# Mixing the last two KV heads of dilated attention: branch weights as 12 rows spread by TensorE in place of rows broadcast by DMA, results left on chip, h fetched last, last maxima fetched by SyncE

## The reference, cut to what matters

```python
for g, (win, dil) in enumerate(BRANCHES):          # ((128, 1), (512, 4), (2048, 16))
    if kv_past is None:
        o, l = dilated_prompt(q[:, :, g], kv_branches[g], win, dil)
    else:
        o, l = dilated_sample(q[:, :, g], kv_branches[g], kv_past[g], win, dil)
    outs.append(o)
    lses.append(l)
wts = jax.nn.softmax(jnp.stack(lses, axis=0), axis=0)
o = jnp.einsum('gnth,gnthe->nthe', wts, jnp.stack(outs, axis=0))
return o.reshape(n, t, ATTN_OUT).astype(h.dtype) @ w_o
```

## Time and profile before

| | |
|---|---|
| median of 3 runs | 2897.13 us (2895.83 to 2897.22) |
| the profiled execution | 2900.13 us, span 2898.4 us |
| TensorE busy | 2710.8 us, 94% of the span |
| VectorE busy | 1365.3 us, 47% |
| ScalarE busy | 832.7 us, 29% |
| sample phase: from the first sample scores to the product with `w_o` | 1884.2 to 2027.0 us, 142.8 us |
| mean granted TensorE clock | 0.958 of full speed |

### The profile page before, as it was taken

One profiled execution on the slowest core, in us unless ns is written; L12 is line 12 of the kernel. 1 busy time (PEld: TensorE's weight loads), 2 busy tenths in 40 slices (PEclk: granted clock), 3 DMA queues, 4 the chain that ended last, 5 costly groups with the idle time before them and its releaser, 6 DMA issues.

```text
span 2898.4 us, 44440 instructions
## 1 busy us (share of the span) xinstructions
PE 2710.8 (94%) x18658; PEld 2577.6 (89%) x18658; DVE 1365.3 (47%) x2255; ACT 832.7 (29%) x1680; POOL 285.0 (10%) x464
## 2 busy tenths in 40 slices
PE   5589999999999999999999999775999999999998
PEld 4489999999999999988888888554999999999998
DVE  8972145423332335666667667534255333233325
ACT  7221132111111113245554544512131111111112
POOL 2300000000000000012422424321000000000000
PEclk8689999999999999999999999867999999999999
DMA  3412111111111111323344454668211111111101
GB/s 95 79 35 59 44 44 44 44 44 43 43 43 43 44 57 53 97 62 84 84 108 129 106 132 112 224 172 272 81 44 44 46 54 40 49 43 43 43 29 61
DMA packets 175567, 215.54 MB, mean 74 GB/s; under 512 B 45894, under 2 KB 128310, under 8 KB 175160
## 3 DMA queue, kind: packets, MB, share of 16 engines
q1 hardware_dynamic: 152960, 161.32, 18.6%
q0 software_dynamic: 22464, 52.23, 7.1%
HBM read 164.86 MB, written 29.92 MB: 67 GB/s over the span
## 4 chain that ended last, share of the span: by engine, by line
PE 73%; DVE 7%; DMA 4%; ACT 3%; issue 3%; POOL 2%; DVEq 0%; POOLq 0%; ACTq 0%
PE PS L221 11%; PE PS L218 11%; PE PS L217 11%; PE PS L396 8%; PE PS L400 8%; PE PS L397 8%; PE PS L2075 4%; PE PS L2076 3%; PE PS L2077 3%; PE PS L2090 2%; DMA CB<-C_SCRATCH 2%; PE PS L2117 2%; PE PS L2104 1%; DVE SQ L191 1%; DVE SSB L2002 1%
## 5 line engine op out<-in xcount | busy, mean ns | idle before, releaser
L217 PE MATMUL PS<-XH,WH 128*128 128x352 f32 x1920 | 617.6, 322 | 3.7 <-PEq L103 3.7
L218 PE MATMUL PS<-XL,WH 128*128 128x352 f32 x1920 | 619.1, 323 | 0.0
L396 PE MATMUL PS<-HIDH,WH 128*128 128x352 f32 x1536 | 494.7, 323 | 8.1 <-DVE HIDL L331 8.1
L397 PE MATMUL PS<-HIDL,WH 128*128 128x352 f32 x1536 | 494.5, 323 | 0.0
L221 PE MATMUL PS<-XH,WL 128*128 128x352 f32 x1920 | 415.0, 324 | 0.0
L217 PEld LDWEIGHTS PS<-XH,WH 128*128 128x128 f32 x1920 | 362.4, 189 | 4.2 <-issue 4.1
L218 PEld LDWEIGHTS PS<-XL,WH 128*128 128x128 f32 x1920 | 361.3, 188 | 0.1
L347 DVE TENSOR_TENSOR H<-PS,H 128x1056 f32<-128x1056 f32 x128 | 160.8, 1256 | 391.6 <-PE PS L400 391.2
L400 PE MATMUL PS<-HIDH,WL 128*128 128x352 f32 x1536 | 331.6, 324 | 0.0
L221 PEld LDWEIGHTS PS<-XH,WL 128*128 128x128 f32 x1920 | 329.4, 188 | 0.0
L396 PEld LDWEIGHTS PS<-HIDH,WH 128*128 128x128 f32 x1536 | 289.2, 188 | 12.7 <-DVE HIDL L331 12.7
(11 more groups left out here) (367 smaller groups left out, 3461.9 us busy)
## 6 DMA issues: line engine op xcount, KB each, us to landing
RAW<-w_up SPq DMA_DIRECT2D x32, 1024.0 KB, 5.3
RAW<-w_down SPq DMA_DIRECT2D x32, 1024.0 KB, 4.9
KVR<-cache_kv_w SPq DMA_DIRECT2D x18, 1024.0 KB, 10.2
QB<-QA SPq DMA_DIRECT2D x120, 132.0 KB, 2.5
ARAW<-w_q SPq DMA_DIRECT2D x24, 512.0 KB, 4.7
O_SCRATCH<-OT POOLq DMA_DIRECT2D x96, 128.0 KB, 2.8
OB<-O_SCRATCH POOLq DMA_DIRECT2D x24, 512.0 KB, 7.0
CB<-C_SCRATCH POOLq DMA_DIRECT2D x48, 256.0 KB, 8.3
```

Of the source, the lines that this page charges most:

```text
L217: nc.tensor.matmul(out, wh(k), xh[:, k, c], start=(k == 0), stop=False)
L218: nc.tensor.matmul(out, wh(k), xl[:, k, c], start=False, stop=False)
L396: nc.tensor.matmul(out, w, m.hidh[:, k, q], start=(k == 0), stop=False)
L397: nc.tensor.matmul(out, w, m.hidl[:, k, q], start=False, stop=False)
```

## The change

Only the mixing of `g` = 2 and 3 (pairs `w` = 4 to 7, now 12 pieces `p`, piece `p` being branch `p % 3` of pair `4 + p // 3`) and what stands around it is changed:

- The weight tile in DRAM is loaded as rows of 512 columns into `CR_RAW` (`pool_rows`: six small loads, 12 rows and, again for the part that full precision loses, 12 more for each half of the columns). ScalarE and VectorE split them into a high and a low part in `CR` (`act_rows`, `dve_rows`). For each piece TensorE multiplies a selection matrix `SEL` with them (`pe_spread`), which spreads a pair's two rows over 128 partitions in a PSUM bank, 2 or 7, half the columns at a time. VectorE multiplies `OB` with the bank (`dve_piece`). The two `CB` loads of each branch are gone.
- Sums of `w` = 4 to 7 stay on chip (`CB` for 4 and 5, `XF` for 6 and 7) and are split from there; their stores to `X_SCRATCH` and loads from it are gone.
- Step by step the pieces stand at steps 0, 1, 2, 4, 5, 6 (`PIECES`), two each. The maxima of `g` = 3 are loaded by SyncE and not by GpSimd, and VectorE uses them at the end of step 1 (before: step 0), the weights at the end of step 2.
- `choose(u-1)` stands before `score(u+1)` and no longer behind the product with V; `keep_o(u-1)` opens VectorE's step. Keys are turned through two banks, and the sample results use bank 6 alone, since banks 2 and 7 are for the pieces.
- SyncE waits only for the last projection before it loads the first five cache tiles, and for the last rotation (`roped`) before the masks. The three `QBL` memsets go from VectorE (steps 84 to 86) to GpSimd (85 to 87). `h` is fetched after `w_o` and later.
- One cache tile (`KVR2`) moves by 512 bytes, and the last tile of step 7 lies in it.

```diff
+    LATE = 2
+    BANKS = (2, 7)
...
+        if g <= self.LATE:
+            self.load_maxima(pool, g, self.ml_in)
+
+    def load_maxima(self, eng, g, sem):
...
     def pool_weights(self, pool, g):
         pool.wait_ge(self.kept, g + 1)
         pool.dma_start(self.s.cd[g], self.s.ct[:]).then_inc(self.ct_out, 16)
-        pool.wait_ge(self.ct_out, 16 * (g + 1))
+        if g < self.LATE:
+            pool.wait_ge(self.ct_out, 16 * (g + 1))
...
+    def adds(self, p):
+        return 2 * (p // 3) + p % 3
+
+    def acc(self, w):
+        return self.s.cb[:, w - 4] if w < 6 else self.s.xf[:, w, 0:SEQ]
+
+    def pool_rows(self, pool, g, free, count):
+        pool.wait_ge(self.ct_out, 16 * (g + 1))
+        pool.wait_ge(free, count)
+        rows = self.s.cd[g].rearrange("(k r) i -> k (r i)", r=8)
+        for e in range(2):
+            for y, n in ((0, 12), (12, 12), (24, 8)):
+                pool.dma_start(self.s.cr_raw[32 * e + y:32 * e + y + n, :], rows[0:n, 512 * e:512 * e + 512]).then_inc(self.rows_in, 16)
+
+    def act_rows(self, act, g):
+        act.wait_ge(self.rows_in, 96 * (g - 1))
+        if g == 3:
+            act.wait_ge(self.spread, 12)
+        self.nc.scalar.activation(self.s.cr[:], self.s.cr_raw[:], ACT.Copy).then_inc(self.row_hi, 1)
...
+    def pool_piece(self, pool, p):
+        s, w, b = self.s, 4 + p // 3, p % 3
+        if p < 2:
+            pool.wait_ge(self.weighed, 11 + p)
+        else:
+            pool.wait_ge(self.taken, 2 * p - 2)
+            pool.wait_ge(self.mixed, self.adds(p - 2))
+        pool.dma_start(s.ob[:, p % 2], s.od[w // 2, b][:, w % 2].rearrange("p t q -> p (t q)")).then_inc(self.b_in[p % 2], 16)
+
+    def pe_spread(self, pe, p):
+        w, b = 4 + p // 3, p % 3
+        pair = 2 * b + w % 2
+        pe.wait_ge(self.rows, w // 2 - 1)
+        for e in range(2):
+            if p:
+                pe.wait_ge(self.taken, 2 * p - 1 + e)
+            rows = slice(32 * e, 32 * e + 24)
+            self.nc.tensor.matmul(self.m.ps[:, self.BANKS[e], :], self.s.sel[rows, pair, :], self.s.cr[rows, :],
+                                  start=True, stop=True).then_inc(self.spread, 1)
+
+    def dve_piece(self, dve, p, free, n):
+        w, b = 4 + p // 3, p % 3
+        acc, ob = self.acc(w), self.s.ob[:, p % 2]
+        dve.wait_ge(self.b_in[p % 2], 48 * 6 + 16 * (p // 2 + 1))
...
+        for e in range(2):
+            dve.wait_ge(self.spread, 2 * p + e + 1)
+            c = self.m.ps[:, self.BANKS[e], :]
...
+            self.nc.vector.tensor_tensor(x if b else half_tiles(acc, b, 0, e), x, c, ALU.mult).then_inc(self.taken, 1)
+        if b:
+            dve.wait_ge(self.taken, 2 * p + 2)
+            dve.wait_ge(self.mixed, self.adds(p) - 1)
+            v = by_tile(acc, b, 0)
+            self.nc.vector.tensor_tensor(v, v, by_tile(ob, b, 1), ALU.add).then_inc(self.mixed, 1)
...
-        if c >= 3:
-            pe.wait_ge(self.kept[self.by_dve(c - 3)], self.before(c - 3))
+        if c >= 2:
+            pe.wait_ge(self.kept[self.by_dve(c - 2)], self.before(c - 2))
...
+PIECES = {0: (0, 1), 1: (2, 3), 2: (4, 5), 4: (6, 7), 5: (8, 9), 6: (10, 11)}
...
     def _(pool):
-        mix.pool_part(pool, 0, 3)
-        for g in (2, 3):
-            for x in range(12 if g == 3 else 13, 31):
-                mix.pool_part(pool, x, g)
+        mix.pool_rows(pool, 2, mix.made, 3)
+        mix.pool_maxima(pool, 3)
+        for p in range(2, 8):
+            mix.pool_piece(pool, p)
+        mix.pool_weights(pool, 3)
+        mix.pool_rows(pool, 3, mix.rows, 1)
+        for p in range(8, 12):
+            mix.pool_piece(pool, p)
...
+            if u in (0, 4):
+                mix.act_rows(act, 2 + u // 4)
             act.wait_ge(neg, u + 1)
...
-        act.wait_ge(pv, 8)
+        act.wait_ge(pv, 7)
         for k in range(KT):
-            act.wait_ge(x_in, 16 * 6 if k < 6 else 16 * 8)
-            nc.scalar.activation(m.xl[:, k, 0:SEQ], s.xf[:, k, 0:SEQ], ACT.Copy).then_inc(x_hi, 1)
-            if k == 0:
+            if k < 4:
+                act.wait_ge(x_in, 16 * 4)
+            else:
+                act.wait_ge(mix.mixed, 2 * (k - 3))
+            nc.scalar.activation(m.xl[:, k, 0:SEQ], result(k), ACT.Copy).then_inc(x_hi, 1)
+            if k == 5:
                 act.wait_ge(placed, 8)
                 nc.scalar.activation(m.xl[:, :, SEQ:NT], s.at_s[:], ACT.Copy).then_inc(s_hi, 1)
```

More of the change, by code:

```diff
@@ L1528, in __init__ @@
         self.weighed, self.added = sig("weighed"), sig("added")
+        self.rows_in, self.row_hi, self.rows, self.sel_made = sig("rows_in"), sig("row_hi"), sig("rows"), sig("sel_made")
+        self.ml_late = sig("ml_late")
+        self.spread, self.taken, self.mixed = sig("spread"), sig("taken"), sig("mixed")
     def pool_maxima(self, pool, g):
@@ L1626, in pool_part @@
             self.pool_maxima(pool, g)
+        elif x == 12 and g == self.LATE:
+            self.pool_weights(pool, g)
+            self.pool_piece(pool, 0)
+            self.pool_piece(pool, 1)
         elif x == 12:
@@ L2155, in sample_phase, with result @@
         "p_turned", "kept_p", "pv", "kept_o", "picked", "placed", "pick_set"))
[L2156 removed]
+    pick_zero, x_in, s_hi, x_hi, x_lo, s_lo = (sig(n) for n in ("pick_zero", "x_in", "s_hi", "x_hi", "x_lo", "s_lo"))
+    s.s_lo = s_lo
     s.h_in, s.x_lo, s.masked, s.kept_p = sig("h_in"), x_lo, masked, kept_p
     tile, tiles = keys_s.tile, keys_s.tiles
+    def result(k):
+        return s.xf[:, k, 0:SEQ] if k < 4 else mix.acc(k)
     def kt(u, n, j, x):
@@ L2185, in _ @@
                     load(u, j)
-            if u < 2:
-                mask(u)
+            if u == 1:
+                sp.wait_ge(s.roped, 3 * N_GR)
+                mask(0)
+                mask(1)
         load(4, 0)
@@ L2292, in place, with low @@
             ins.then_inc(placed, 1)
+        def low(k):
+            dve.wait_ge(x_hi, k + 1)
+            nc.vector.tensor_tensor(m.xh[:, k, 0:SEQ], result(k), f32(m.xl[:, k, 0:SEQ]), ALU.subtract).then_inc(x_lo, 1)
+        mix.dve_choice(dve)
         for u in range(8):
+            if u:
+                keep_o(u - 1)
             if u + 1 < 8:
@@ L2312, in _ @@
             nc.vector.tensor_scalar(s.spr[:, u % 2, :], s.spr[:, u % 2, :], s.sst[:, 3, u:u + 1], None, ALU.mult).then_inc(normed, 1)
[L2313 to L2317 removed]
+            if u:
+                place(u - 1)
+            if u in (0, 4):
+                mix.dve_rows(dve, 2 + u // 4)
+            for p in PIECES.get(u, ()):
+                mix.dve_piece(dve, p, *((mix.x_out, 16 * (p // 3 + 3)) if p < 6 else (pv, 2)))
+            if u == 1:
                 mix.dve_maxima(dve, 3)
[L2319 to L2321 removed]
+            if u == 2:
                 mix.dve_weights(dve, 3)
[L2323 to L2326 removed]
+        wo.lo(dve, 0)
+        low(0)
         keep_o(7)
[L2328 to L2330 removed]
+        low(1)
         place(7)
[L2332 to L2337 removed]
+        for k in range(2, 4):
+            low(k)
+        dve.wait_ge(s_hi, 1)
+        nc.vector.tensor_tensor(m.xh[:, :, SEQ:NT], s.at_s[:], f32(m.xl[:, :, SEQ:NT]), ALU.subtract).then_inc(s_lo, 1)
+        for k in range(4, KT):
+            low(k)
         wo.lo(dve, 1)
@@ L2384, in _ @@
                 turn_k(u + 1)
+            if u:
+                choose(u - 1)
+            if u + 1 < 8:
                 score(u + 1)
```

133 lines of the change are left out of this document (73 added, 60 removed).

## The result

The changed kernel takes 2861.49 us (median of 4 runs, 2859.75 to 2863.20) against 2896.48 us of the kernel before (4 runs beside them): the ratio is 0.9879, 95% interval 0.9864 to 0.9893. The profiled execution took 2860.89 us, its span is 2859.1 us where it was 2898.4.

A forecast was written before the change was run, and what follows sets the result against it. Transfers were taken to bound the sample phase, through VectorE's order. Gains of 10 + 5.3 + 21.3 + 0.7 = 37.3 us, against 2 and 3.3 lost, gave 32: profiled execution 2868 us, median 2865, range 2853 to 2882.

The forecast's parts named there:

- the steps: Sample phase, six steps from the second turning of probabilities: 72.8 us in sum where it was 94.1, gain 21.3.
- the further stretch at half speed: Sample phase: one more stretch of some 12 us at half speed from rests in steps with pieces, 3.3 us lost.
- the product's start: First product with `w_o`: may run at half speed longer after a longer TensorE rest, 2 us lost (0 to 5).
- the start: From the sample phase's start T: probabilities normalised at T+15.8, step 1's turned at T+30 where it was T+35.3; gain 5.3 us.
- the end: Last turning of probabilities to the product with `w_o`: 12.6 us where it was 13.3, gain 0.7.
- the tail: Attention tail ahead of the sample phase: `OT` stall 7.3, memsets 2.2, half-speed work 0.5; gain 10 us, bounds 3 and 12.
- What bounds the phase: Sample phase: transfers bound it through VectorE's order, with waits of 46.9 us for `CB` and 14.1 us for maxima.
- The spread: TensorE's two spreads of 512 columns in a step: cost 0.4 us at full speed and 0.9 at half.
- The clock: TensorE's clock: if recent activity as a whole releases half rate, steps stay at full speed, time about 2861 us.
- half speed stays: Rival, sample phase: rests of 1 to 2 us keep half speed, steps take 15.5 us each; 2882 us, chance 0.14.
- the stores stay late: Rival, attention tail: earlier cache tiles still cover the stores of `OT`, tail gives 2 us; 2873 us, chance 0.14.
- Late rows: Rival, steps 0 and 4: row loads take 8 us, not 3.1, ScalarE stands 5 us longer; 2875 us, chance 0.08.

The follow-up runs named there:

- the maxima part alone: Kernel before, with only the maxima of `g` = 3 loaded by SyncE and used one step later, `CB` loads kept: 2885.65 us, 0.9956.
- the run with both: Changed kernel plus row copies of the `CB` loads' bytes to DRAM and SyncE's old wait for the last rotation: 2865.04 us, 0.9876.
- the second profile: Profile of the changed kernel run once more with no edit: 2858.95 us, 0.9860.
- the last version: Changed kernel with memsets on VectorE, rows copied behind the exponential at steps 0 and 4, and the six last pieces later: 2852.10 us, 0.9838.
- every load twice: Changed kernel with each `OB` load of pieces 2 to 11 done twice, the second starting when the first has landed: 2876.95 us, 0.9925.
- rows behind the exponential: Changed kernel with ScalarE's wait for and copy of the weight rows moved behind the exponential at steps 0 and 4: 2856.41 us, 0.9851.

## Why the prediction was right

The median was forecast at 2865 us and is 2861.5, inside 2853 to 2882; the mechanism of the phase was the one of the forecast. Several terms were off, and the two that went the other way bring the number nearer by luck: against the 2868 us forecast for the profiled execution (2860.9) the steps gave 3.1 us more, the further stretch at half speed 3.3, the product's start 2.4, the start 1.7 and the end 0.6, while the tail gave 2.2 less and the program ahead of it took 1.7 more by chance.

- *What bounds the phase.* Right: the waits for `CB` and for the maxima are gone and the phase gives 32.8 us. The runs add shares: the maxima part alone gives 10.4 us; row copies of the same bytes, asked for in good time, cost 1 to 2 us (3 in the run with both); and a second load behind the first costs 18.5.
- *The attention tail.* Forecast 10 us, measured 7.8. The 7.3 us stall went, as said. The cause given for it was not shown: half the queue and the cache tiles' start, put back singly and together, do not restore it, and `h` was not fetched there, while the kernel that keeps the `CB` loads keeps it. What of those loads does it (their destination in SBUF, or the `OB` load that stood behind the weight store and not ahead of it) stays open. The term with the wrong sign is the one behind it: "The three `QBL` memsets leave VectorE ... I take 2.2 us". I had bounded it by 0 and 5 and so had excluded a loss; the move costs 0.6 to 1.5 us by the run that takes it back.
- *The start.* Forecast the first two turnings at T+15.8 and T+30, measured T+14.9 and T+28.3. The rows were there at T+12.8 and not T+13.6: the six loads were issued at 1885.61 to 1888.65 (T+7.5 on) and ScalarE's copy began at 1890.92, 2.3 us behind the end of the last issue, though the median landing of the rows of 24 KB is 3.8 us.
- *The steps.* Forecast 10.8, 13.0, 14.0, 14.8, 10.5, 9.7 (72.8 us); measured 10.4, 12.4, 13.9, 13.4, 10.3, 9.3 (69.7). The sum of rows was right to 0.1 to 0.6 us in five of six. Step 4 ran at half speed behind the rows' rest as forecast, but for 7.7 us only, hence 13.4.
- *The spread.* Estimated 0.4 us at full and 0.9 at half, measured 0.50 and 0.79.
- *The end.* 12.6 us forecast, 12.0 measured (12.9 in the second profile).
- *The two deductions.* The 3.3 us were for one more stretch at half speed "since each step with pieces has rests of 0.8 and 0.5 to 1.6 us". No such rest lowered the clock in steps 1 to 3 or 5. A further stretch did come at the end, from 1974.7 us on, behind a rest of 3.03 us that the forecast did not have: two pieces stand on VectorE ahead of the copy that `choose` needs. The run with the last piece one step later prices it at 2.6 us. Its cost lies in the last two stages, which were still 0.4 and 0.6 us shorter than forecast. The 2 us for the start of the product did not show: the clock is 0.57 from 1990 to 1992 and 1.00 from 1992, 3.6 us of half speed where it was 4.9 before (0.50 from 2027 to 2031, full from 2032), but 5.7 in the second profile; what follows the phase takes 871.0 and 872.3 us where it took 871.4.
- *The clock.* The prediction's paragraph on the Trainium skill ("TensorE: Matmul & The Clock Gate", Part 1) gave about 2861 us, and the median is 2861.5; with the terms above off by as much, that agreement is no proof. For that reading speaks that the steps stayed at full speed through their rests of 0.4 to 0.8 us; the rest of 3.72 us had half speed with it all the same.

Of the rivals, *half speed stays* would have shown steps of 15.5 us, *the stores stay late* waits of ScalarE for `OT`; neither is there. *Late rows* happened in part: one of the prediction's own signs of being wrong, a wait of ScalarE for the rows over 5 us, is there (5.43 us at step 4), yet TensorE's rest behind it was 3.72 us and the step 13.9, as forecast. Of the signs of being right, the product began 110.0 us behind the first sample scores and not 118, and these came at 1878.1 and not near 1874, since the tail gave less and the program ahead of it took longer.

## What to carry to other kernels

Where an engine in the middle waits for a transfer that can be asked for only when that engine has given a buffer back, count the transfers in the chain and the moment of the request before the bytes: here 6 MB asked for in good time cost some 4 us in all, and one more transfer in each piece's chain 18.5. When work is moved off a busy engine to an idle one, look for what the two share; a memset on GpSimd held up VectorE by 1.95 us (2.12 for 0.17), where on VectorE it had taken 1.76. A rest that can't be removed is best put behind work that TensorE has ready, and pieces spread so that no step has two of them ahead of its critical copy.

## What I had not expected of the hardware

- A VectorE scaling of 0.17 us lasts until the end of a GpSimd memset that runs beside it (2.12 us), and eight short memsets in a row hold it as long as one long one (2.43 us). A copy from PSUM beside the same kind of memset keeps its 0.69 us.
- The length of a single rest did not decide the clock. A rest of 2.31 us (the last version) and one of 1.78 (every load twice) left full speed, while with the last piece later the clock fell 0.5 us behind a rest of 1.19, and the rest of 2.35 us there lies within that stretch at half. Behind 3.01 us (rows behind the exponential) the spread still took 0.50 us, as at full, and only the product after it was at half (0.97 and 2.79 us for 0.67 and 1.50).
- How long half speed lasted varied too, against the 12 us that I had taken: 13.7 us at the start of the phase (1885.9 to 1899.6), 10.3 at step 4, of which the last 7.7 with work (to 1950.8), and 3.4 at the same place with the rows behind the exponential.
- Sixteen loads of 4 KB on SyncE's queue were issued from 1891.1 to 1901.8 without any engine's wait behind them; on GpSimd's they were part of 14.1 us.
- The copies of rows from DRAM to DRAM (256 KB each) landed in 7.1 us in the tail, where the loads of the same rows into `CB` took 12.6 in the kernel before (medians of four). The cause was not found.
